# C's attention on one core: the sample's four jobs are placed ahead of the prompt's tiles

## The reference, cut to what matters

```
def _chunk_causal_prompt(q, k, v, scale):      # blocks of 128 queries, i = 0..7
    qchunk = (i * QBLOCK + jnp.arange(QBLOCK)) // CHUNK
    mask = (kchunk[None, :] <= qchunk[:, None])[None]
    return _attend(qi, k, v, mask, scale)      # softmax(q k * scale) v
...
oc = _full_attend(cq[:, :, :, None], ck, kv[..., C_NOPE:], C_QK ** -0.5, q_start, prompt)
```

## Time and profile before

| what | value |
|---|---|
| median of three runs | 3183.57 us |
| the profiled execution's own time | 3183.15 us |
| its span, first to last instruction | 3181.2 us |
| mean granted TensorE clock | 0.944 |
| TensorE: matmul busy, weight load busy | 2900.1 us (91%), 2742.6 us (86%) |
| VectorE, ScalarE, GpSimd busy | 1747.1, 1204.0, 126.0 us |
| C's attention stage, layer 0 | 602.8 to 691.2 us |
| C's attention stage, layer 1 | 2165.8 to 2258.6 us |

### The profile page before, as it was taken

How to read it: one execution, slowest core, us unless ns; L and a number is a source line. 1 busy time by engine, 2 the same in 40 slices (tenths; PEclk the granted TensorE clock), 3 DMA queues, 4 the chain that set the end, 5 groups by cost and what they waited for, 6 DMA issues and landing times. The chain is left out here.

```text
span 3181.2 us, 49151 instructions
## 1 busy us (share of the span) xinstructions
PE 2900.1 (91%) x19106; PEld 2742.6 (86%) x19106; DVE 1747.1 (55%) x2837; ACT 1204.0 (38%) x2563; POOL 126.0 (4%) x248
## 2 busy tenths in 40 slices
PE   6888879899999999999978878789899999999997
PEld 5686868589999999999967768667899999999997
DVE  3467764743655555555645496466436555545554
ACT  5556544652322222222246574456423222221223
POOL 0200012000000000000001000120000000000000
PEclk8996989899999999999989889898899999999999
DMA  4110001121111111111031100101311111111111
GB/s 180 54 41 29 22 27 40 50 103 40 47 47 40 47 46 40 46 53 43 17 140 48 46 15 19 44 25 51 119 34 47 47 40 47 47 45 46 40 52 57
DMA packets 182256, 160.90 MB, mean 51 GB/s; under 512 B 14504, under 2 KB 169912, under 8 KB 181560
## 3 DMA queue, kind: packets, MB, share of 16 engines
q1 hardware_dynamic: 182072, 158.46, 15.7%
HBM read 129.57 MB, written 29.06 MB: 50 GB/s over the span
## 5 line engine op out<-in xcount | busy, mean ns | idle before, releaser
L1888 PE MATMUL ps<-h_hi,w_hi 128*128 128x352 f32 x2496 | 546.8, 327 | 20.7 <-DVE w_lo L1997 11.2
L1888 PE MATMUL ps<-h_hi,w_lo 128*128 128x352 f32 x2496 | 541.5, 324 | 0.0
L1888 PE MATMUL ps<-h_lo,w_hi 128*128 128x352 f32 x2496 | 541.4, 325 | 0.0
L1888 PEld LDWEIGHTS ps<-h_hi,w_hi 128*128 128x128 f32 x2496 | 428.1, 191 | 25.5 <-DVE w_lo L1997 11.6
L1888 PEld LDWEIGHTS ps<-h_hi,w_lo 128*128 128x128 f32 x2496 | 431.8, 189 | 0.0
L1888 PEld LDWEIGHTS ps<-h_lo,w_hi 128*128 128x128 f32 x2496 | 427.7, 189 | 0.0
L2331 ACT ACTIVATE cv<-up,cols 128x1058 f32<-128x1058 f32 x88 | 112.1, 1274 | 718.8 <-issue 678.7
L783 PE MATMUL ps<-w_hi,h_hi 128*128 128x256 f32 (+1 forms) x1088 | 316.5, 291 | 21.8 <-DVE w_lo L1011 20.0
L784 PE MATMUL ps<-w_lo,h_hi 128*128 128x256 f32 (+1 forms) x1088 | 310.8, 286 | 0.0
L2440 DVE TENSOR_TENSOR x_t<-ps,x_t 128x1056 f32<-128x1056 f32 x176 | 220.9, 1255 | 160.9 <-PE ps L1888 160.1
L785 PE MATMUL ps<-w_hi,h_lo 128*128 128x256 f32 (+1 forms) x1088 | 308.7, 284 | 0.0
(11 more groups left out here) (234 smaller groups left out, 4287.5 us busy)
## 6 DMA issues: line engine op xcount, KB each, us to landing
stage<-in_f_win SPq DMA_DIRECT2D x88, 512.0 KB, 3.7
stage<-in_f_wout SPq DMA_DIRECT2D x44, 512.0 KB, 3.6
stage<-in_w_in SPq DMA_DIRECT2D x40, 256.0 KB, 3.8
x_spill<-x_t SPq DMA_DIRECT2D x2, 4224.0 KB, 13.2
x_t<-x_spill SPq DMA_DIRECT2D x2, 4224.0 KB
w_raw<-in_w_in SPq DMA_DIRECT2D x24, 256.0 KB, 4.1
stage<-in_w_o SPq DMA_DIRECT2D x12, 512.0 KB, 4.0
o_raw<-o_spill SPq DMA_DIRECT2D x8, 528.0 KB, 5.0
```

Of the source, the lines that this page charges most:

```text
L1888: last = pe.matmul(ps[:, s0 + b, 0:BAND], lh, rh_[:, b * BAND:(b + 1) * BAND], start=(first_k and n == 0), stop=(last_k and n == 2))
```

## The change

C's attention is given the list of tiles 8, 0, 1, ... 7 in place of 0, 1, ... 8. The same list goes to `single_jobs`, which makes the jobs, and to `attention_stage`, where SyncE's sends follow it. So the sample's jobs become 0 to 3 and the prompt's 4 to 35. Job numbers at which `prepare` acts stay 12, 16, 20 and 24; they now fall on tiles 2, 3, 4 and 5 in place of 3, 4, 5 and 6.

```
     def attention_c(prepare):
-        return attention_stage(single_jobs(4, lambda h: h, kc_s), lambda kt: v_big[:, kt, :],
+        tiles = [PT_TILES] + list(range(PT_TILES))
+        return attention_stage(single_jobs(4, lambda h: h, kc_s, tiles), lambda kt: v_big[:, kt, :],
                                lambda h: [(2 * h, 2 * h), (2 * h, 2 * h + 1), (2 * h + 1, 2 * h)], 96,
-                               Region(R_W2 + 17408, R_END), tok=256, prepare=prepare)
+                               Region(R_W2 + 17408, R_END), tok=256, tiles=tiles, prepare=prepare)
```

## The result

The changed kernel took 3220.13 us (median of 4 runs, 3218.63 to 3221.55) and the kernel before, beside it, 3184.27 us (4 runs, 3183.4 to 3185.77): a ratio of 1.0112 with the interval [1.0092, 1.0131], some 36 us slower. I had forecast 3194.1 us and a range up to 3199.5 us. The direction was right and the size was not. The profiled execution took 3218.85 us, 35.7 us more than that of before. Further down, two executions that ran far longer than all others (4078.08 us in experiment one, 12161.61 us in experiment three) are left out of the ratios.

The account below looks back on a forecast made before the run. TensorE was taken to bound C's stage, at half clock in front. Per layer, 13.6 us added in front, less 8.1 or 9.2 at the end, plus 0.3, gave +10.5 us together: 3194.1 us, range 3180.5 to 3199.5.

Parts of the forecast that it names:

- What bounds the stage: C's stage: TensorE bounds it, at half its clock in the front and at the full clock in the rest.
- Part 1: End of C's stage: removing the sample's jobs gives back 8.1 us in layer 0 and 9.2 us in layer 1.
- Part 2: Front of C's stage: the sample's four jobs at 1.2 GHz add 13.6 us a layer, bounds 8.1 and 17.4.
- the score product: Sample's jobs in the front: 0.44 us for each product of 544 keys, three a job, 1.32 us.
- the wait for exponentials: Behind the sample's first scores in the front: 0.5 us, bounds 0 to 1.2, as two jobs fit the banks.
- Part 3: Last send and conversions: the larger send adds 0.3 us a layer; moved conversions taken as nothing, bounds 0 to 1.3 us.
- the one step that this sum stood on: C's front: the clock returns at the same point of the prompt's work as before; chance 0.50.
- Rival (c): Tiles 2 and 3 of C: clock returns later than now, +19 us at most, 3198 to 3202 us; chance 0.12.
- does little for the clock: Sample's jobs in B's stage and layer 1 of C: low clock there read as these jobs doing little for it.
- (a): C's front: clock returns at the same time after the start, 11.0 and 18.1 us; +3.0 us, 3186.6 us; chance 0.20.
- (b): C's front: the sample's dense scores bring the clock back early; -3.7 us, 3179.9 us; chance 0.18.

Follow-up runs that it names:

- experiment one: Added ScalarE copies ahead of C's stage: kernel before with two 3183.67 us, with four 3194.16 us; changed kernel with two 3211.18 us.
- experiment three: 20 unread matmuls added ahead of C's stage: kernel before 3180.11 us, changed kernel 3215.01 us, sample between tiles 3 and 4 3185.23 us.
- ninth: Changed kernel with the sample's jobs in their own block and a barrier before the prompt's tiles: 3198.99 us, ratio 1.0004 to the kernel before.
- sixth experiment: Changed kernel with its first four jobs taking 128 query columns in place of 32: median 3204.59 us, ratio 1.0071 to the kernel before.

## Why the prediction was right or wrong

**What bounds the stage: right.** TensorE bounds it throughout, at either clock.

**Part 1, the end: right.** The stage gives back 8.09 and 9.20 us; I had 8.1 and 9.2. The end of layer 1, columns as in the earlier trace rows; layer 0's is the same:

```profile
2289.25 0.93 PE L1331 MATMUL ps<-ident,prob 128*128 128x128 f32 x7
...
2289.90 3.65 PEld L1345 LDWEIGHTS ps<-v_big,pt 128*128 128x128 f32 x32
...
2293.73 0.28 DVE L1266 TENSOR_SCALAR osb<-ps,rden 128x64 f32<-128x64 f32 x1 [1.51 <-PE ps L1345]
...
2294.05 0.32 SPq L1545 DMA_DIRECT2D o_tok_spill<-osb  x1
...
2296.97 0.37 SPq L1931 DMA_DIRECT2D o_tok<-o_tok_spill  x1
```

No transposes stand between the last two jobs' values (32 loads in one row), a single copy follows, and nothing waits for exponentials.

**Part 2, the front: right in kind, 10% low.** I had 13.6 us; it is 14.95. One term at fault is the score product. I took 0.44 us for one with 544 keys from B; the third and fourth job of C, six products, take 610.50 - 607.51 = 2.99 us, 0.50 each. For twelve products this is 0.7 us more. The first two jobs take 607.51 - 604.25 = 3.26 us, 0.27 more for the wait for exponentials, where I had 0.5. Transposes and values are as I had them, 1.96 us a job. The other 0.9 us lies in the prompt's own first work, for which I had nothing: eight score sets of tiles 0 and 1 with tile 0's transposes and values, 7.21 us in the kernel before, take 8.1 us between the sample's.

**Part 3: right.** The time from the last copy to the next block grows by 0.03 us in layer 0 and 0.23 us in layer 1; I had 0.3. The conversions cost nothing that shows.

**The sum at an unchanged clock** would so be 2 x 14.95 - 8.09 - 9.20 + 0.26 = +12.9 us against my +10.5, near 3196 us and within the forecast's own range.

**What failed is the one step that this sum stood on**, "The sum holds the release of the clock at its place in the prompt's work". It cost 26.2 us in layer 0 and 1.2 us in layer 1. Counted by the scores issued, its place was tile 2's second job in layer 0 and tile 3's first in layer 1 (tile 2 ends there after 8.5 us, so that "10.9 us into it" was misread); it came in tile 5's last job and in tile 3's second. Rival (c) named the mechanism, a later return, and then bounded it by the end of tile 3, +19 us, which nothing in the trace supported. The evidence for more was on the table: B, the one stage that has the sample's narrow jobs in its front, had been at 0.50 for 48 us. I had read that row and let it argue for "does little for the clock" rather than for "keeps it away". It is no clean example, though: I wrote that a busy TensorE was held at 0.50 for up to 48 us, but in B's stage it is busy for 8.00 of 8.00 us only from 260 to 268 us, and for 5.07 of 8 us before that and 11.47 of 16 behind. A spread like B's, worked through, gives the sizes measured: the slow tiles advance by 3.20, 4.40 and 5.12 us a job in place of 1.69, 2.34 and 2.71, for each tile of four jobs 6.0, 8.2 and 9.6 us. And 0.12 was far too small a chance for the only case of which the trace held an example. The range ended at 3199.5 us for that reason. That layer 1 lost only 1.2 us doesn't bear the step out: in another execution of the same kernel that layer had its clock back after 83.0 us.

**Rivals (a) and (b) fell.** A return at a fixed time, and an early one by the dense scores, did not occur in any of ten stretches with the sample first. Rival (b) had beside it the page "TensorE: Matmul & The Clock Gate" of the Trainium skill, "What's actually happening". It says that sustained activity releases the throttle. The trace does not bear that out: TensorE was busy for 67.0 of 67.0 us (620 to 687 us) at 0.50.

**What was shown, and what was not.** Shown by runs: the loss is time at the low clock, not added waits (the profile after); it comes with the sample's jobs in front (tile 3 and tile 4 first don't lose, the sample in the middle doesn't); with a barrier between them and the prompt the loss of clock in the prompt's work is gone (ninth); neither a shift of the start nor the place of the conversions makes one order into the other. Suggested by one execution and not shown: that they pull down a clock that is up (third; in the middle they did not). That it is the 32 columns, rather than another trait of these jobs, rests on the sixth experiment's two stages, with a median that only half follows. Left open: why the clock, once away, stays away through whole tiles of full-width work, long after the last narrow matmul (its load lies ahead of 622.6 us; the return is at 687 us), while it is back after 4.5 us when the stage starts with tile 3's jobs; why the sample's jobs do no harm in the middle; and what picks one of the several times of return in otherwise equal executions.

## What to carry to other kernels

When small, narrow TensorE work is to be moved in front of wide work, read the granted clock first, and look for a stage of the same kernel that already has that order: its time at the low level is the price to put in, not a footnote. Price a return of the clock as a spread over several tiles, since a few microseconds of its shift are worth more than all the instructions moved here. Where a stage starts at the low level, try full-width jobs of middle length first: tile 3 first took 0.4% off this kernel, with one list changed, and tile 4 first took nothing that could be told. And read more than one profiled execution: the same instructions in front had their clock back after 11.0 us in one and after 29.0 in another.

## What the runs showed of the hardware

- TensorE at 100% busy stayed at half clock for 67 us on end (620 to 687 us in the changed kernel), for the last 64 us with full-width weights and up to 768 keys a job. The busy share alone does not tell the clock.
- Within a stream of 32-column score products and their small transposes and values at the stage's start, with TensorE busy for 6.09 of 7.50 us, a granted clock of 0.99 fell to 0.50, in both layers of one execution. The same jobs among those of tiles 3 and 4, with TensorE busy for 18.40 of 18.40 us, kept 1.00.
- The return of the clock recurs at a few times in the same stage: 11, 18.5, 20.5 and 29.5 us prompt first, 26.5, 35.5 to 36, 44.5, 66 and 83 us sample first. The time of an unchanged kernel varies with the clock: the kernel before ran from 3171.92 us (mean granted clock 0.948) to 3193.69 us (0.941) over 23 executions on one chip, and from 3180.72 us (0.945) to 3219.28 us (0.931) over 25 on another.
- Full clock through all of C's stage is worth 4.3 / 8.5 us (87.0 / 87.0 against 91.3 / 95.5), and yet 20 to 31 unread matmuls that hold it gave no median gain beyond doubt.
